# Attention by pairs of heads in a six-layer kernel, with four score banks and the bias added in PSUM

## Chip, cores and metric

The kernel runs on one core of a Trainium2 chip. The metric is the device time of one execution in microseconds (us), lower is better. The core's engines are TensorE (PE, matrix products), VectorE (DVE), ScalarE (ACT), GpSimd (POOL) and SyncE (SP, which issues the weight loads). They run side by side and meet at semaphores. Matrix products are written to PSUM, which has eight banks here: `acc0` to `acc3`, `prod0`, `prod1`, `stat0`, `stat1`.

## What is computed

A stack of six layers on 256 tokens of width 1024, all in float32: each layer is half a SwiGLU feed-forward (2816 hidden), a mixer, and another half feed-forward. The mixers are, in order, gated linear attention, neighbourhood attention (NA), latent attention (MLA), gated linear attention, and twice four branches, of which two are attentions. Four mixers hold a softmax attention, and those are what the change touches:

```python
# NA, 16 heads of 64: a bias per pair of positions, NEG_INF outside the window
s = jnp.einsum('bqhd,brkhd->bhqrk', q_r, k_blk) * NA_HEAD_DIM ** -0.5
p = softmax(where(mask, s + bias, NEG_INF));  o = p @ v
# MLA, 16 heads: 64 plain and 32 rotated dimensions, no mask, no bias
s = jnp.einsum('bqhd,bkhd->bhqk', q, k) * (64 + 32) ** -0.5
p = softmax(s);  o = p @ v                       # v has 64 columns a head
# branches: 4 sliding-window heads with a bias and a sink
p = exp(s - m) / (sum(exp(s - m)) + exp(sink - m))
# and 4 forgetting heads: s + (cum_q - cum_k), causal
```

## The kernel before

All weights come as slabs of 1 MB (`raw`, three buffers), each of which ScalarE rounds to its high part (`split`, L853) and VectorE reduces to the low rest (`low_of`, L1132). A projection multiplies high by high, high by low and low by high in fp32r (`three`, L404 to L406) into a `prod` bank; the feed-forward sums go to the `acc` banks. The attention has no weights: it runs in plain float32, where every matmul is issued as two passes of the array.

The order of the work is written out by hand, one instruction stream for each engine. The mixers `na`, `mla` and `branches` of each engine first run the projections and norms of queries, keys and values, then call that engine's `attention`, and then the output projection. In all of them 256 queries are two tiles of 128 (`tt`), and 256 keys are two tiles (`kt`).

`attention` on TensorE (L565 to L594) loops over `i` in `heads + 3` steps. Step `i` waits for the scaled probabilities of head `i-2` (`p_ready`, L570), writes the scores of head `i` to `acc[i % 2]` (L575; two query tiles, one term each in NA, two terms in MLA with 64 and with 32 rows, three terms in the forgetting heads with 64, 4 and 4 rows), transposes the probabilities of head `i-2` to `acc[2 + h % 2]` (L582), and multiplies the values of head `i-3` by the transposed probabilities (L592) into one half of a `stat` bank: even heads fill partitions 0 to 63, odd ones 64 to 127. A head with an even number has its queries and keys on partitions 0 to 63, one with an odd number on 64 to 127 (`half64`).

VectorE's `attention` (L1317) does for head `i`: scale and bias of the scores (L1330), from `acc` to a `logits` buffer, then the maximum (L1334 or L1337); in MLA a maximum of `acc` (L1325) and its product with the scale (L1326). Then for head `i-1`: the reciprocal of the sum (L1345) and two multiplications of the probabilities (L1347), which signal `p_ready`. Every other step it takes the low rest of a finished pair of outputs (`low_out`, L1360). In the branches it also does the gates' remaining work between steps (`operands`, L1667).

ScalarE's `attention` (L918) copies the transposed probabilities out of PSUM (L926), computes the exponentials with their sums (L932, from `logits`, or in MLA from `acc`), the sink's exponential (L935), and the high part of a pair of outputs (L941).

Before NA's attention VectorE still has two slab rests to do, and before that of the branches one gate and a slab rest (`lows`).

Of the kernel before, what the change touches and what calls it, by code (L numbers as in the profile page):

```python
# [15 lines left out]
P = 128  # L16
# [114 lines left out]
def build(nc, W, PRM, CST, START, RPB, XIN, OUT, TOE_ROWS, TOE):  # L131
    ctx = ExitStack()
    with ctx:
# [35 lines left out]
        small = sb("small", [P, 4, 8])  # L169
# [107 lines left out]
        def half64(h):  # L277
            return slice(64 * (h % 2), 64 * (h % 2) + 64)
# [19 lines left out]
        def attention_buffers(at, rest, i):  # L298
            return [[bits(at, 0), bits(at, 1)], [bits(at, 2), bits(at, 3)], [bits(rest, i), bits(rest, i + 1)]]
# [93 lines left out]
        def _(pe):  # L393
# [171 lines left out]
            def attention(kind, heads, scores, values):  # L565

                _, probs, probsT = buffers[kind]
                for i in range(heads + 3):
                    if 2 <= i < heads + 2:
                        pe.wait_ge(p_ready, c.up(p_ready))  # L570
                    if i < heads:
                        for tt in range(TT):
                            pairs = scores(i, tt)
                            for n, (lhs, rhs) in enumerate(pairs):
                                last = nc.tensor.matmul(acc[i % 2][:, tt, :], lhs, rhs, start=(n == 0),  # L575
                                                        stop=(n == len(pairs) - 1))
                        last.then_inc(s_done, 1)
                    if 2 <= i < heads + 2:
                        h = i - 2
                        for kt in range(TT):  # L580
                            for tt in range(TT):
                                last = nc.tensor.transpose(acc[2 + h % 2][:, kt, tt * P:(tt + 1) * P],  # L582
                                                           probs[h % 2][:, tt, kt * P:(kt + 1) * P], ident)
                        last.then_inc(t_done, 1)
                    if i >= 3:
                        h = i - 3
                        if h % 2 == 0 and h >= 4:
                            pe.wait_ge(ot_ready, ot_base + h // 2 - 1)
                        pe.wait_ge(pt_ready, c.up(pt_ready))
                        half = slice(64 * (h % 2), 64 * (h % 2) + 64)  # L590
                        for kt in range(TT):
                            last = nc.tensor.matmul(stat[h // 2 % 2][half, 0, :], values(h, kt), probsT[h % 2][:, kt, :],  # L592
                                                    start=(kt == 0), stop=(kt == TT - 1))
                        last.then_inc(pv_done, 1)  # L594

# [230 lines left out]
        def _(act):  # L826
# [91 lines left out]
            def attention(heads, scale, kind, sink=None):  # L918

                out = xh if kind == "branches" else oh  # L920
                logits, probs, probsT = buffers[kind]
                tables("natural_log_exp_and_others")
                for i in range(heads + 3):
                    if 2 <= i < heads + 2:
                        act.wait_ge(t_done, c.up(t_done))
                        nc.scalar.activation(probsT[i % 2][:, :, :], acc[2 + i % 2][:, :, :], ACT.Copy).then_inc(pt_ready, 1)  # L926
                    if i < heads:
                        act.wait_ge(logits_ready, c.up(logits_ready))
                        st = small[:, i % 2, :]
                        src = acc[i % 2] if scale else logits[i % 2]  # L930
                        for tt in range(TT):
                            last = nc.scalar.activation(probs[i % 2][:, tt, :], src[:, tt, :], ACT.Exp, bias=st[:, tt:tt + 1],  # L932
# [1054 lines left out]
```

## Time and profile before

| | us |
|---|---|
| median of 3 runs | 3887.76 (3886.63 to 3892.89) |
| the profiled execution | 3889.2 |
| its span in the trace | 3887.4 |

| engine | busy us | share of the span |
|---|---|---|
| TensorE, matmul | 3635.3 | 94% |
| TensorE, weight load | 3445.8 | 89% |
| VectorE | 2591.0 | 67% |
| ScalarE | 1495.6 | 38% |
| GpSimd | 7.0 | 0% |

The profile is of one execution. A matmul's record is longer than the distance to the next, since matmuls are pipelined; the distance between starts is what a matmul costs in a row of them. The granted clock is TensorE's share of its full speed: 1.00 is 2.4 GHz, 0.50 is 1.2 GHz; over the span it is 0.952. In every view a line number is that of the code above, an arrow names what ended the idle time, and the shapes are partitions times elements. A float32 matmul of the attention appears as two records, one for each pass.

### The profile page before, as it was taken

To read this page: it belongs to the slowest core of one execution; us is meant where nothing else is said; L and a number is where in the kernel's file an instruction comes from. 1 tells how busy PE (TensorE), PEld (TensorE's weight loads), DVE (VectorE), ACT (ScalarE), POOL (GpSimd) and SP (SyncE) were. 2 spreads that over 40 slices of the span, in tenths; PEclk is the share of its full clock that TensorE was granted. 3 is DMA by queue.
4 is the path that set the end of the run, shared out by engine and by line. 5 is a ranking of instruction groups with operands and counts; after the bars stand their busy time and mean duration, and the time that the engine had idled before them with its cause. 6 is when DMAs were issued, how large, how long until landed. Compare 5 with 4: busy or idle time off the path is not lost.

```text
span 3887.4 us, 65961 instructions
## 1 busy us (share of the span) xinstructions
PE 3635.3 (94%) x27625; PEld 3445.8 (89%) x27625; DVE 2591.0 (67%) x2987; ACT 1495.6 (38%) x1446; POOL 7.0 (0%) x6
## 2 busy tenths in 40 slices
PE   8998899997999986999999889999888999988899
PEld 8997799995899986499999879999867999987799
DVE  7678767676667667266767876766766666676565
ACT  4343334343434343243434233434343343444243
POOL 0000000000000000000000000000000000000000
PEclk9999999998999998699999989999988999998899
DMA  6542374542354442035555225454432545543154
GB/s 240 183 179 82 120 216 173 183 152 98 109 183 176 180 162 87 0 141 183 176 180 182 90 88 191 175 185 173 163 120 85 186 173 186 183 161 141 65 184 162
DMA packets 98919, 592.68 MB, mean 152 GB/s; under 512 B 25684, under 2 KB 26836, under 8 KB 27736
## 3 DMA queue, kind: packets, MB, share of 16 engines
q1 hardware_dynamic: 97280, 586.41, 42.3%
q10 hardware_dynamic: 1496, 4.20, 0.3%
q8 instruction: 109, 1.79, 0.2%
q14 instruction: 34, 0.28, 0.0%
HBM read 588.47 MB, written 2.11 MB: 152 GB/s over the span
## 4 chain that ended last, share of the span: by engine, by line
PE 80%; DVE 13%; issue 4%; ACT 3%; DMA 1%; SPq 0%; DVEq 0%; ACTq 0%
PE prod L404 18%; PE prod L406 18%; PE prod L405 18%; PE acc L404 7%; PE acc L406 6%; PE acc L405 6%; PE acc L575 3%; DVE low L1132 3%; ACT high L853 2%; DVE work L1426 1%; PE stat L592 1%; DVE work L1627 1%; DVE work L1419 1%; PE acc L582 1%; DVE newt L1166 1%
## 5 line engine op out<-in xcount | busy, mean ns | idle before, releaser
L404 PE MATMUL prod<-xh,high 128*128 128x256 f32 x5968 | 1710.9, 287 | 45.9 <-DVE gs L1690 12.8
L405 PE MATMUL prod<-xl,high 128*128 128x256 f32 x5968 | 1691.5, 283 | 0.0
L406 PE MATMUL prod<-xh,low 128*128 128x256 f32 x5968 | 1684.9, 282 | 0.0
L1132 DVE TENSOR_TENSOR low<-raw,high 128x2048 fp32r<-128x2048 f32 x537 | 1231.9, 2295 | 559.6 <-ACT high L853 555.3
L853 ACT ACTIVATE high<-raw 128x2048 fp32r<-128x2048 f32 x550 | 1047.7, 1908 | 950.0 <-PE prod L406 486.1
L404 PEld LDWEIGHTS prod<-xh,high 128*128 128x128 f32 x5968 | 1128.4, 189 | 64.3 <-issue 25.6
L406 PEld LDWEIGHTS prod<-xh,low 128*128 128x128 f32 x5968 | 1137.8, 191 | 0.0
L405 PEld LDWEIGHTS prod<-xl,high 128*128 128x128 f32 x5968 | 1131.4, 190 | 4.1 <-issue 3.1
L404 PE MATMUL acc<-ends,high 128*128 128x256 f32 x2112 | 597.8, 283 | 0.4 <-DVE low L1132 0.4
L405 PE MATMUL acc<-ends,high 128*128 128x256 f32 x2112 | 596.6, 282 | 0.0
L406 PE MATMUL acc<-ends,low 128*128 128x256 f32 x2112 | 591.9, 280 | 0.0
L406 PEld LDWEIGHTS acc<-ends,low 128*128 128x128 f32 x2112 | 401.7, 190 | 0.0
L405 PEld LDWEIGHTS acc<-ends,high 128*128 128x128 f32 x2112 | 396.4, 188 | 0.0
L404 PEld LDWEIGHTS acc<-ends,high 128*128 128x128 f32 x2112 | 394.9, 187 | 0.6 <-issue 0.6
L910 ACT ACTIVATE sg<-gs 128x512 f32<-128x512 f32 x120 | 76.0, 634 | 561.0 <-DVE gs L1281 561.0
L1281 DVE TENSOR_TENSOR gs<-prod,rstd 128x512 f32<-128x512 f32 x120 | 83.0, 691 | 162.7 <-PE prod L406 162.6
L575 PE MATMUL acc<-work 64*128 64x256 f32 (+1 forms) x256 | 109.9, 563 | 51.3 <-DVE work L1347 42.8
L1247 DVE TENSOR_TENSOR sg<-sg,gs 128x512 f32<-128x512 f32 x132 | 92.1, 698 | 93.2 <-ACT sg L910 84.0
L575 PEld LDWEIGHTS acc<-work 64*128 64x128 f32 (+1 forms) x256 | 52.4, 253 | 108.6 <-DVE work L1347 60.2
L404 PE MATMUL prod<-ends,high 128*128 128x256 f32 x384 | 114.0, 297 | 30.7 <-DVE ends L1458 19.0
L405 PE MATMUL prod<-ends,high 128*128 128x256 f32 x384 | 112.8, 294 | 0.0
L406 PE MATMUL prod<-ends,low 128*128 128x256 f32 x384 | 112.7, 293 | 0.0
(194 smaller groups left out, 2772.6 us busy)
## 6 DMA issues: line engine op xcount, KB each, us to landing
raw<-stream SPq DMA_DIRECT2D x550, 1024.0 KB, 4.8
work<-rpb SPq DMA_DIRECT2D x16, 256.0 KB, 6.6
work<-bias_shifted ACTq DMA_DIRECT2D x2, 1024.0 KB, 5.3
cst<-consts SPq DMA_DIRECT2D x1, 1122.0 KB, 11.5
x<-x_in SPq DMA_DIRECT2D x1, 1024.0 KB, 5.0
raw<-stream SPq DMA_DIRECT2D x2, 512.0 KB, 7.0
work<-bias_by_distance ACTq DMA_DIRECT2D x2, 512.0 KB, 4.6
bias_shifted<-work ACTq DMA_DIRECT2D x1, 1024.0 KB, 5.8
```

The costliest lines, as they stand in the source:

```text
L404: nc.tensor.matmul(out, wh, ah, start=start, stop=False, **kw)
L405: nc.tensor.matmul(out, wh, al, start=False, stop=False, **kw)
L406: return nc.tensor.matmul(out, wl, ah, start=False, stop=stop, **kw)
L575: last = nc.tensor.matmul(acc[i % 2][:, tt, :], lhs, rhs, start=(n == 0), stop=(n == len(pairs) - 1))
L582: last = nc.tensor.transpose(acc[2 + h % 2][:, kt, tt * P:(tt + 1) * P], probs[h % 2][:, tt, kt * P:(kt + 1) * P], ident)
L592: last = nc.tensor.matmul(stat[h // 2 % 2][half, 0, :], values(h, kt), probsT[h % 2][:, kt, :], start=(kt == 0), stop=(kt == TT - 1))
L853: nc.scalar.activation(high[:, s % HIGH, :], raw[:, s % RAW, :], ACT.Copy).then_inc(high_ready, 1)
L910: nc.scalar.activation(sg[:, :, :], gs[:, :, :], ACT.Sigmoid).then_inc(sig_ready, 1)
L1132: v.tensor_tensor(low[:, s % LOW, :], raw[:, s % RAW, :], high[:, s % HIGH, :].bitcast(F32), ALU.subtract).then_inc(low_ready, 1)
L1166: link(v.tensor_tensor(t, t, w, ALU.mult))
L1247: v.tensor_tensor(sg[:, :, :], sg[:, :, :], gs[:, :, :], ALU.mult).then_inc(vec_step, 1)
L1281: v.tensor_tensor(gs[:, :, :], prod[0][:, :, :], over(rstd[:, :], 2), ALU.mult).then_inc(evac, 1)
```

## The change

- The three `attention` functions loop over pairs of heads. On TensorE, step `i` writes the scores of pair `i`, then the values of pair `i-3`, then the transposes of pair `i-2`. Scores and values are issued alternately for the two heads of the pair: term by term for scores, key tile by key tile for values.
- Scores go to four banks, `acc[2 * (i % 2) + u]`. They wait for the exponentials of pair `i-2` (`exp_done`), no longer for its scaled probabilities. Transposes go to `prod[u]`; for that TensorE waits at the start for all projections to be taken out of `prod` (`evac`).
- The probabilities have four buffers, and `small` eight rows. The `logits` buffers are gone: scale and bias are written back to the same PSUM bank, from which the maximum and the exponentials are read.
- In MLA the scale goes into the norm of the queries (`variance(..., factor)`), so that the maximum is taken with `negate=True` and no product follows.
- Output copies and `low_out` follow each pair step, the last three `low_out` after the loop. `operands(i)` is now called at pair steps.

```diff
-        small = sb("small", [P, 4, 8])
+        small = sb("small", [P, 8, 8])
...
-            return [[bits(at, 0), bits(at, 1)], [bits(at, 2), bits(at, 3)], [bits(rest, i), bits(rest, i + 1)]]
+            return [bits(at, j) for j in range(4)], [bits(rest, i), bits(rest, i + 1)]
...
@@ TensorE, in place of L567 to L594
+                probs, probsT = buffers[kind]
+                pairs = heads // 2
+                pe.wait_ge(evac, n_prod[0])
+                exps = c.now(exp_done)
+                c.up(exp_done, heads)
+                for i in range(pairs + 3):
+                    if i < pairs:
+                        if i >= 2:
+                            pe.wait_ge(exp_done, exps + 2 * (i - 1))
+                        terms = len(scores(2 * i, 0))
+                        for tt in range(TT):
+                            for n in range(terms):
+                                for u in range(2):
+                                    lhs, rhs = scores(2 * i + u, tt)[n]
+                                    last = nc.tensor.matmul(acc[2 * (i % 2) + u][:, tt, :], lhs, rhs, start=(n == 0),
+                                                            stop=(n == terms - 1))
+                                    if tt == TT - 1 and n == terms - 1:
+                                        last.then_inc(s_done, 1)
+                    if i >= 3:
+                        pair = i - 3
+                        if pair >= 2:
+                            pe.wait_ge(ot_ready, ot_base + pair - 1)
+                        pe.wait_ge(pt_ready, c.up(pt_ready, 2))
+                        for kt in range(TT):
+                            for u in range(2):
+                                last = nc.tensor.matmul(stat[pair % 2][half64(u), 0, :], values(2 * pair + u, kt), probsT[u][:, kt, :],
+                                                        start=(kt == 0), stop=(kt == TT - 1))
+                        last.then_inc(pv_done, 1)
+                    if 2 <= i < pairs + 2:
+                        for u in range(2):
+                            pe.wait_ge(p_ready, c.up(p_ready))
+                            for kt in range(TT):
+                                for tt in range(TT):
+                                    last = nc.tensor.transpose(prod[u][:, kt, tt * P:(tt + 1) * P],
+                                                               probs[(2 * (i - 2) + u) % 4][:, tt, kt * P:(kt + 1) * P], ident)
+                            last.then_inc(t_done, 1)
@@ ScalarE, in place of L922 to L941
+                pairs = heads // 2
+                for i in range(pairs + 3):
+                    for u in range(2):
+                        h = 2 * i + u
+                        if 2 <= i < pairs + 2:
+                            act.wait_ge(t_done, c.up(t_done))
+                            nc.scalar.activation(probsT[u], prod[u][:, :, :], ACT.Copy).then_inc(pt_ready, 1)
+                        if i < pairs:
+                            act.wait_ge(logits_ready, c.up(logits_ready))
+                            st = small[:, h % 4, :]
+                            for tt in range(TT):
+                                last = nc.scalar.activation(probs[h % 4][:, tt, :], acc[h % 4][:, tt, :], ACT.Exp, bias=st[:, tt:tt + 1],
+                                                            accum_out=st[:, 2 + tt:3 + tt])
...
+                            last.then_inc(exp_done, 1)
                     if i >= 3:
                         act.wait_ge(pv_done, c.up(pv_done))
...
+                        nc.scalar.activation(out[:, i - 3, :], stat[(i - 3) % 2][:, 0, :], ACT.Copy).then_inc(ot_high, 1)
@@ VectorE, in place of L1319 to L1355
+                def largest(h):
+                    st, mx, b = small[:, h % 4, :], small[:, 4 + h % 4, 0:2], acc[h % 4][:, :, :]
+                    dve.wait_ge(s_done, c.up(s_done))
+                    if bias is not None:
+                        added = bias(h)
+                        k = added.shape[-1]
+                        rows = b.rearrange("p a (r k) -> p (a r) k", k=k)
+                        link(v.scalar_tensor_tensor(rows, rows, scale, added, ALU.mult, ALU.add))
...
+                        v.tensor_reduce(st[:, 0:2], b, AX_X, ALU.max, negate=True).then_inc(logits_ready, 1)
+
+                def shares(h):
+                    st = small[:, h % 4, :]
+                    dve.wait_ge(exp_done, c.up(exp_done))
...
+                    link(v.reciprocal(st[:, 6:8], st[:, 2:4]))
+                    for tt in range(TT):
+                        last = v.tensor_scalar(probs[h % 4][:, tt, :], probs[h % 4][:, tt, :], st[:, 6 + tt:7 + tt], None, ALU.mult)
+                    last.then_inc(p_ready, 1)
+
+                for i in range(pairs + 1):
+                    for u in range(2):
+                        if i < pairs:
+                            largest(2 * i + u)
+                        if i >= 1:
+                            shares(2 * (i - 1) + u)
+                    if i >= 4:
+                        low_out(i - 4, out)
                     if between:
                         between(i)
+                for pair in range(pairs - 3, pairs):
+                    low_out(pair, out)
...
-                    qs = (variance(2 * T, NOPE + ROPE), variance(T, NOPE + ROPE))
+                    scale = 1.0 if keys else float(NOPE + ROPE)
+                    qs = (variance(2 * T, NOPE + ROPE, scale), variance(T, NOPE + ROPE, scale))
```

## Rows read from the trace of the kernel before

**Rows 1.** The page's chain of waits: share of the span by line.

```profile
PE prod L404 18%; PE prod L406 18%; PE prod L405 18%; PE acc L404 7%; PE acc L406 6%; PE acc L405 6%; PE acc L575 3%; DVE low L1132 3%; ACT high L853 2%; DVE work L1426 1%; PE stat L592 1%; DVE work L1627 1%; DVE work L1419 1%; PE acc L582 1%; DVE newt L1166 1%
```

**Rows 2.** Window table: us, busy of PE, PEld, DVE, ACT, POOL; PEclk, DMA, GB/s.

```profile
932.60:998.70 66.10, 48.53 (x193) 27.46 (x192) 41.79 (x92) 31.11 (x89) 0.00 (x0) 0.85 0.11 41
957.30:998.70 41.40, 33.47 (x151) 18.85 (x150) 26.35 (x66) 21.90 (x64) 0.00 (x0) 1.00 0.00 0
1557.50:1661.80 104.30, 100.59 (x257) 47.10 (x257) 27.59 (x88) 27.35 (x88) 0.00 (x0) 0.62 0.00 0
1557.50:1605.70 48.20, 45.79 (x94) 20.97 (x94) 10.44 (x33) 10.36 (x35) 0.00 (x0) 0.50 0.00 0
2877.00:2934.90 57.90, 44.64 (x131) 23.89 (x129) 27.24 (x60) 19.59 (x52) 0.00 (x0) 0.65 0.12 44
3570.40:3628.00 57.60, 44.35 (x130) 23.67 (x129) 27.21 (x60) 19.81 (x52) 0.00 (x0) 0.64 0.13 45
```

**Rows 3.** Chain in order of time in NA: start us, length us, what.

```profile
961.33 0.70 DVE work L1330
...
962.06 0.69 DVE small L1337
...
962.85 0.62 DVE work L1347 x2
...
963.52 1.14 PE acc L575 x4
...
964.69 0.70 DVE work L1330
```

**Rows 4.** Timeline in NA: start us, length us, engine, line, operation, tiles, idle before.

```profile
960.03 0.42 DVE L1360 TENSOR_TENSOR ends<-stat,ends 128x256 fp32r<-128x256 f32 x1
...
961.23 0.66 PE L582 MATMUL acc<-cst,work 128*128 128x128 f32 x4
...
961.81 1.08 PE L592 MATMUL stat<-work 128*64 128x256 f32 x4
961.98 0.60 ACT L926 ACTIVATE work<-acc 128x512 f32<-128x512 f32 x1 [1.46 <-PE acc L582]
...
962.78 0.51 ACT L932 ACTIVATE work<-work,small 128x256 f32<-128x256 f32 x1 [0.20 <-DVE small L1337]
```

**Rows 5.** Timeline where NA's attention begins.

```profile
932.66 1.14 PE L575 MATMUL acc<-work 64*128 64x256 f32 x8
...
938.75 0.68 DVE L1330 SCALAR_TENSOR_TENSOR work<-acc,work 128x512 f32<-128x512 f32 x1
```

**Rows 6.** Chain in order of time in NA at half clock.

```profile
946.55 2.07 PE acc L575 x4
...
949.66 1.90 PE stat L592 x4
```

**Rows 7.** Chain in order of time in MLA at half clock.

```profile
1589.99 4.59 PE acc L575 x8
1594.58 1.04 PE acc L582 x4
1595.62 1.90 PE stat L592 x4
```

**Rows 8.** Chain in order of time in MLA at full clock.

```profile
1609.62 2.57 PE acc L575 x8
```

**Rows 9.** Groups by line in MLA: maximum taken from PSUM.

```profile
L1325 DVE TENSOR_REDUCE small<-acc 128x2 f32<-128x512 f32 x16 | 11.1, 691 | 71.2 <-PE acc L575 71.2
```

**Rows 10.** Groups by line in NA: maximum taken from SBUF.

```profile
L1337 DVE TENSOR_REDUCE small<-work 128x2 f32<-128x512 f32 x16 | 11.0, 686 | 0.5
```

**Rows 11.** Chain in a branches layer: scores of forgetting heads, half and full clock.

```profile
2914.19 6.29 PE acc L575 x12
...
2923.43 3.37 PE acc L575 x12
```

**Rows 12.** Timeline in a branches layer: TensorE's second scores.

```profile
2888.83 2.07 PE L575 MATMUL acc<-work 64*128 64x256 f32 x4 [10.63 <-DVE work L1347]
```

More of the change, by code:

```diff
@@ L565, in attention @@
             def attention(kind, heads, scores, values):
[L567 to L571, printed above, removed]
-                        for tt in range(TT):
[L573 to L579, printed above, removed]
-                        for kt in range(TT):
[L581 to L593, printed above, removed]
-                        last.then_inc(pv_done, 1)
@@ L916, in ffn, with attention @@
                 ahead(s0 + FFN_SLABS - 1)
-            def attention(heads, scale, kind, sink=None):
+            def attention(heads, kind, sink=None):
                 out = xh if kind == "branches" else oh
-                logits, probs, probsT = buffers[kind]
+                probs, probsT = buffers[kind]
                 tables("natural_log_exp_and_others")
[L923 to L932, printed above, removed]
-                                                        scale=scale or 1.0, accum_out=st[:, 2 + tt:3 + tt])
-                        if sink is not None and i < SWA_HEADS:
-                            last = nc.scalar.activation(st[:, 4:6], st[:, 0:2], ACT.Exp, bias=sink(i))
-                        last.then_inc(exp_done, 1)
@@ new lines, in attention @@
+                pairs = heads // 2
[11 more added lines that the diff above has]
+                                                            accum_out=st[:, 2 + tt:3 + tt])
+                            if sink is not None and h < SWA_HEADS:
+                                last = nc.scalar.activation(st[:, 4:6], st[:, 0:2], ACT.Exp, bias=sink(h))
+                            last.then_inc(exp_done, 1)
@@ L993, in na @@
                 ahead(s + 8, 4)
-                attention(NA_HEADS, None, "na")
+                attention(NA_HEADS, "na")
                 complete(gain, evac, s + 12)
@@ L1148, in half_low, with variance @@
                                 ALU.subtract).then_inc(signal, 1)
-            def variance(width, n):
+            def variance(width, n, factor=1.0):
                 q = n_stat[0] % 2
@@ new lines, in attention @@
+                probs, _ = buffers[kind]
+                pairs = heads // 2
+                def largest(h):
[6 more added lines that the diff above has]
+                        link(v.scalar_tensor_tensor(rows, rows, scale, added, ALU.mult, ALU.add))
+                    if sink is not None and h < SWA_HEADS:
+                        link(v.tensor_reduce(mx, b, AX_X, ALU.max))
+                        v.tensor_scalar(st[:, 0:2], mx, sink(h), -1.0, ALU.max, ALU.mult).then_inc(logits_ready, 1)
+                    else:
+                        v.tensor_reduce(st[:, 0:2], b, AX_X, ALU.max, negate=True).then_inc(logits_ready, 1)
```

54 lines of the change are left out of this document (9 added, 45 removed).

## Prediction

> **What bounds the kernel now.** I read the page's chain of waits first: most of the span is TensorE in the fp32r projections (the lines of `three`), which this change does not touch. The attention lines L575, L582 and L592 hold about 5% of the chain, with the VectorE work between them [rows 1]. So I went to the stages. The window table gives four attention stretches: neighbourhood attention (NA) 66.1 us, MLA 104.3, and the two branches layers 57.9 and 57.6, together 285.9 us [rows 2]. DMA is idle in most of them and the slabs for the next projection are already split, so time saved here should reach the end.
>
> They have three different limits. In NA at full clock a serial loop between two engines sets the pace: bias add 961.33, maximum 962.06, shares 962.85, next scores 963.52, and the next bias add 964.69, 3.36 us a head, of which 2.2 VectorE and 1.1 TensorE [rows 3]. `wait_ge(p_ready)` ahead of `scores` makes that loop: TensorE does not issue scores until VectorE has scaled the head two before. In MLA TensorE never stops: 4.59 us scores, 1.04 transposes, 1.90 values a head, 7.53 in all at half clock [rows 7]; the granted clock is 0.50 for the first 48.2 us [rows 2]. The branches mix both; at half clock a forgetting head's scores take 6.29 us, at full 3.37 [rows 11].
>
> **The scores.** Heads 2i and 2i+1 lie in rows 0-63 and 64-127 of the array. At the start of NA two heads' scores are queued together: eight passes in 1.14 us [rows 5], where four passes of one head later take 1.14 as well [rows 3]. Two heads overlap completely when nothing stands between them. The change makes every pair like that, so I price a pair's scores at one head's: 1.14 us at full clock, 2.07 at half [rows 6]. The other end is no overlap, twice as much; I take full overlap because a row shows it for the same shapes.
>
> The Trainium skill (TensorE: Matmul & The Clock Gate, Part 3) says that tiles in different row groups overlap but that matmuls start in program order. By that rule heads issued one after the other would not start together, as they do in [rows 5]; the row decides, and in alternating order both would overlap anyway, with 5 pass times where 4 are counted here, some 2 us on MLA.
>
> MLA's scores change tile height (64 rows, then 32) four times a head; 4.59/4 = 1.15 us each [rows 7], and even its first two heads cannot overlap. After, all terms of equal height of a pair stand together: four such steps a pair and not eight, each with two heads at once. A pair's scores are then 4.59 us at half clock, 2.57 at full [rows 7, 8]. The forgetting heads' two 4-row terms use the same rows for both heads and stay serial; of 6.29 us, 2 x 1.15 is the 64-row term and 4.0 the others. A pair has 2 x (1.15 + 2.0 + four further passes at 0.45) = 9.9 us for 12.6, at full clock 5.1 for 6.7 [rows 11].
>
> **Transposes and values.** Transposes stay 1.04 us a head at half clock [rows 7] and about 0.6 at full (four recorded in 0.66, [rows 4]); only their bank moves to `prod`. A pair's values, alternating between column halves 0-63 and 64-127 of one bank, have no overlapping example in this trace: 1.90 us (both at once) to 3.8 (serial) at half clock [rows 6], 1.08 to 2.0 at full [rows 4]. I take overlap, by nearness to the row halves. (The Trainium skill, TensorEngine Tiling (Array Packing), Key Properties, has tiles running in parallel; no run here shows it for columns.) A TensorE pair is thus 1.14+1.2+1.08 = 3.4 (4.3 serial) us at full clock in NA, 2.07+2.08+1.9 = 6.1 (8.0) at half; in MLA 2.57+1.2+1.0 = 4.8 (5.8), or 4.59+2.08+1.9 = 8.6 (10.5).
>
> **VectorE and ScalarE.** With two pairs of lead and four score banks VectorE no longer waits for the scores it has just released. Its step a pair in NA is two heads at 2.14 us (961.33 to the end of 962.85) plus `low_out` 0.42 = 4.7 us [rows 3, 4]. MLA drops one tiny VectorE product a head by putting the factor 96 into the variance: no gain, since TensorE is the bound; a VectorE pair there, without bias adds, is 4.7 - 2 x 0.7 = 3.3. ScalarE has four exponentials of 0.51, two copies of 0.60 and small ones (sums, output) that I put at 0.6, 3.8 us a pair [rows 4], below either bound. The bias add now writes its PSUM bank and the maximum reads PSUM. No row shows VectorE writing PSUM; reading PSUM and writing SBUF is 691 ns. Bounds of -0.1 to +0.1 us a bias add, times 32, are -3 to +3 us on the path; I take zero. A maximum from PSUM takes 691 ns [rows 9] against 686 from SBUF [rows 10]: 32 x 5 ns is nothing.
>
> The Trainium skill (VectorE: DVE Perf Modes, the TRN2 errata) charges 62 cycles more for a PSUM source than for an SBUF one. This speaks against the change: 32 maxima x 65 ns would be an estimated 2 us. The two rows disagree with it.
>
> **Waits added.** `evac` at the start, because `prod` now takes transposes: behind it stand the first two pairs' scores, for which VectorE waits; VectorE is busy with slab lows until 938.75 anyway [rows 5], so it is hidden, and would cost about 2 us a stage without them. `exp_done` before scores holds transposes and values queued behind it, but it is for the pair two back and long done when VectorE or TensorE is the bound. `pt_ready` of values now stands ahead of the transposes; ScalarE has a scores time to finish the copies: hidden, or 0.5 us a pair at full clock in MLA (0 to 4 us, taken as 0).
>
> **The sum, by stage.** NA: VectorE starts 6.1 us into the stage, eight steps of 4.7 = 37.6, then transposes, copy, values, copy and `low_out` 3.3: 47. TensorE begins at half clock after its idle time, as now; there its 6.1 us outrun the 4.7, I add 2: 49 for 66.1, gain 17. MLA: 8 x 4.8 + 4 for fill and tail = 42 at full clock. I let the first 20 us be at half clock, +10: 52 for 104.3, gain 52. Branches: TensorE is idle until 2888.8, when the first shares come [rows 12]; I keep that. All at half clock, 2 x 9.9 + 4 x 2.08 + 4 x 1.9 + 2 = 38, end 2926.5 for 2934.9, gain 8. At full clock VectorE decides: its 27.2 us of work in the stage [rows 2] all stay, with some 10 of waits at the two ends 37, gain 21. Between them 14, twice 28. Together 17 + 52 + 28 = 97 us off the profiled execution's 3889.2 (span 3887.4): 3792; the median is 1.4 lower, so 3791.
>
> **The clock** is the largest unknown. What the rows show: NA reaches 1.00 at 957.3 after working gaplessly at half clock since about 946 and keeps it for 41.4 us, although TensorE then waits each head; MLA stays at 0.50 for 48.2 us though TensorE is busy 45.8 of them [rows 2]. The differences are 32-row terms and the gaps of height changes. After the change the same passes run in about 0.57 of the time, two at once, denser than NA's today. That is why I let it rise.
>
> The Trainium skill (TensorE: Matmul & The Clock Gate, Part 1) says activity releases the half clock. MLA contradicts that as it stands; by the rule the outcome is rival F below.
>
> **Rivals.**
> (A) As above, 3791: 0.42.
> (B) Column halves do not overlap: NA is still covered (4.3 under 4.7), MLA loses 8 x 1.0, each branches layer 3: 3791 + 14 = 3805: 0.15. For: no row shows it. Against: row halves do.
> (C) The clock stays at half in MLA and the forgetting heads. MLA 8 x 8.6 + 6 = 75, gain 29; branches 2 x 8; NA 17: 62 us, 3826: 0.27. For: the 48.2 us. Against: denser work.
> (D) The change does not do what it says, scores do not overlap in alternation. NA hardly suffers (4.5 against 4.7), MLA 8 x 7.4 + 12 = 71, gain 33, branches 8 each: 3889 - 66 = 3822: 0.04.
> (E) Slower: each switch between row or column halves drains the array as MLA's height changes do, 1.15 us for two passes at half clock [rows 7], and the clock stays there. NA's pair is 4.6 + 2.1 + 4.6 = 11.3 us, stage 98; MLA 9.2 + 2.1 + 4.6 = 15.9, stage 133; branches +10 each: +81 us, 3969. It turns slower where a TensorE pair passes about 7 us in NA and 12.5 in MLA. Against: eight passes in 1.14 us. 0.03.
>
> (F) MLA runs at full clock from its first scores on, 42 us and not 52: 3781, 0.09. For: its first scores are packed as densely as any later ones. Against: the stage starts at half clock now [rows 2]. (The same is what the Trainium skill's page on TensorE, named above, would lead to.)
>
> **Range.** All at full clock gives 19 + 62 + 42 = 123 us, 3765, the lower end. Upward C is taken in, with half the price of B at half clock (15): 3840. Left out are C with B in full, and E. A alone reaches from 3765 to 3808. About 0.2% (8 us) can be told from no change: faster 0.96, same 0.01, slower 0.03.
>
> **What would show it.** Scores of a pair: eight passes in 1.14 us. MLA's scores: 16 passes in 2.6 (4.6) us for two heads, and its granted clock. Values: eight passes in 1.1 or in 1.9 us. NA: bias adds of a pair every 4.7 us with no wait for L575's successor. The bias add's mean near 691 ns. Wrong would be a MLA stage above 75 us, a VectorE wait for scores in the middle of NA, or a changed time outside the four stages.

## The result, and the profile after

The changed kernel takes 3799.21 us (median of four runs, 3797.88 to 3802.74) where the kernel before takes 3889.13 (3886.63 to 3892.89): ratio 0.9769, 95% interval 0.9752 to 0.9786. The prediction was 3791 with a range of 3765 to 3840. The profiled execution after is 3797.88 us long, its span 3796.1 for 3887.4 before, so 91.3 us went.

Where they went is read by one rule for all kernels here: an attention stage runs from the start of the last projection matmul before it to the start of the first one behind it. For MLA this takes in some 45 us of norms and small sums ahead of the scores, the same in both kernels.

| us | before | after | gone |
|---|---|---|---|
| NA | 66.4 | 48.5 | 17.8 |
| MLA | 149.9 | 94.1 | 55.8 |
| branches, first | 58.0 | 48.4 | 9.7 |
| branches, second | 57.8 | 45.1 | 12.7 |
| all the rest | 3555.4 | 3560.0 | -4.6 |

The window table of the changed kernel (NA, the first projections behind it, MLA in two parts, the forgetting heads of the first branches layer, the second branches layer; columns as in [rows 2]):

```profile
933.50:981.70 48.20, 29.08 (x193) 18.73 (x192) 40.68 (x92) 28.36 (x89) 0.00 (x0) 0.89 0.14 52
981.70:986.70 5.00, 4.98 (x29) 4.98 (x30) 0.00 (x0) 0.00 (x0) 0.00 (x0) 0.66 0.01 3
1542.00:1559.00 17.00, 16.95 (x62) 8.16 (x62) 6.61 (x18) 5.93 (x23) 0.00 (x0) 0.50 0.01 1
1559.00:1590.90 31.90, 27.58 (x198) 15.86 (x196) 17.82 (x54) 19.94 (x67) 0.00 (x0) 1.00 0.00 1
...
2818.60:2849.00 30.40, 29.09 (x88) 18.21 (x88) 16.49 (x47) 9.11 (x33) 0.00 (x0) 0.50 0.00 1
...
3492.70:3534.70 42.00, 31.01 (x129) 19.95 (x129) 24.34 (x58) 18.18 (x52) 0.00 (x0) 0.67 0.14 51
```

In NA, TensorE's busy time fell from 48.5 us [rows 2] to 29.1 with the same 193 matmul records: most of that is the overlap of pairs, a part of it the higher granted clock (0.89 for 0.85). VectorE's stayed near 41, now of a stage of 48.2. In MLA the granted clock is 0.50 for 17 us, not 48.2, and then 1.00 to the end. In the first branches layer it is 0.50 while the forgetting heads run.

The chain of waits of the changed kernel in NA, in order of time (start us, length us, what); it answers to [rows 3]:

```profile
959.11 0.62 DVE acc L1338
...
959.75 0.69 DVE small L1343
...
960.55 0.62 DVE work L1352 x2
961.16 0.62 DVE acc L1338
...
963.22 0.33 DVE ends L1371
963.55 0.61 DVE acc L1338
...
972.10 0.34 DVE ends L1371
...
972.48 1.97 PE stat L592 x8
974.46 1.06 PE prod L600 x4
975.54 1.09 ACT work L937 x2
```

The scores are gone from the chain: VectorE goes from bias add to maximum to shares of two heads and `low_out` without a wait, and a pair takes 4.44 us (959.11 to 963.55). Before, one head took 3.36. But after VectorE's last step that has scores to work on, which ends at 972.10, a tail begins in which TensorE, ScalarE and VectorE work by turns, until the next projection at 981.72.

The same view in MLA (L581 scores, L600 transposes, L592 values, L937 ScalarE's copy of the transposes); it answers to [rows 7, 8]:

```profile
1542.05 13.91 PE acc L581 x48
...
1557.85 3.13 PE acc L581 x16
1560.99 1.01 PE stat L592 x8
1562.00 1.02 PE prod L600 x8
1563.03 2.53 PE acc L581 x16
...
1576.72 2.53 PE acc L581 x16
1579.24 1.01 PE stat L592 x8
...
1588.90 1.10 PE stat L592 x8
```

Sixteen score passes, two heads, take 2.53 us at full clock, where eight passes of one head took 2.57 [rows 8]. Eight passes of values take 1.01.

### The profile page after: what moved, and what is told of

Same layout as the page of the kernel before. It is cut to its first block, busy times and chain, and to the rows that moved or that the text cites. A ratio compares the mean times of both kernels' runs of the same rounds, so it can differ in the third digit from the quotient of the medians.

```text
span 3796.1 us, 65923 instructions
## 1 busy us (share of the span) xinstructions
PE 3547.5 (93%) x27625; PEld 3418.4 (90%) x27625; DVE 2586.0 (68%) x2971; ACT 1488.5 (39%) x1446; POOL 7.4 (0%) x6
## 4 chain that ended last, share of the span: by engine, by line
PE 79%; DVE 13%; issue 4%; ACT 4%; DMA 1%; SPq 0%; DVEq 0%; ACTq 0%
PE prod L404 19%; PE prod L405 18%; PE prod L406 18%; PE acc L404 7%; PE acc L405 7%; PE acc L406 7%; DVE low L1140 3%; ACT high L861 2%; PE acc L581 2%; DVE work L1437 1%; DVE work L1639 1%; DVE work L1430 1%; DVE newt L1174 1%; DVE newt L1173 1%; PE stat L592 1%
## 5 line engine op out<-in xcount | busy, mean ns | idle before, releaser
L404 PE MATMUL prod<-xh,high 128*128 128x256 f32 x5968 | 1711.5, 287 | 46.2 <-DVE gs L1702 13.2
L878 ACT ACTIVATE xh<-x,prm 128x256 fp32r<-128x256 f32 x140 | 63.6, 502 | 121.1 <-DVE x L1242 115.9
L404 PEld LDWEIGHTS prod<-ends,high 128*128 128x128 f32 x384 | 78.2, 204 | 34.3 <-DVE ends L1469 21.3
```

What stands on the lines that cost most here:

```text
L404: nc.tensor.matmul(out, wh, ah, start=start, stop=False, **kw)
L878: return nc.scalar.activation(xh[:, k, :], x[:, k, :], ACT.Identity, scale=par(gain, k))
```

## The experiments

All of them are read against the kernel before that ran beside them (3888.6 to 3890.5 us). The stages are measured as in the table above.

**The lead without the pairs.** The kernel before, with its order of heads, its banks and its VectorE work.

```diff
+                exps = c.now(exp_done)
+                c.up(exp_done, heads)
                 for i in range(heads + 3):
-                    if 2 <= i < heads + 2:
-                        pe.wait_ge(p_ready, c.up(p_ready))
+                    if 2 <= i < heads:
+                        pe.wait_ge(exp_done, exps + i - 1)
...
                     if 2 <= i < heads + 2:
                         h = i - 2
+                        pe.wait_ge(p_ready, c.up(p_ready))
```

> The kernel before with one part of the change: scores of head i wait for the exponentials of head i-2 (exp_done) and the wait for the scaled probabilities (p_ready) stands ahead of the transposes. No pairs, no four banks, no alternation. Theory 'three limits': only NA has the serial loop that this opens; there TensorE's own 2.7 us a head (1.06 + 0.59 + 1.08) becomes the pace in place of 3.36, about 10 us off the stage of 66; MLA stays near 104 us at half clock, since TensorE never stopped there; the branches 1 to 4 us each; in all 12 to 18 us, 3871 to 3877. Rival 'the lead is what counts': most of the 90 us come back here, 3815 or below.

Measured: 3854.98 us, ratio 0.9919 (0.9903 to 0.9936). NA 54.6, MLA 131.2, branches 54.9 and 53.1. That is 33.8 us off, where 12 to 18 were expected and the rival wanted more than 70: neither forecast held. NA and the branches are about as expected, but MLA, expected to keep its time, lost 18.7 us. The profiled execution is the fastest of four (3849.57 to 3863.01 us), so its stages may show more than the others had. Window table of this kernel's MLA scores, and its chain of waits:

```profile
1545.70:1584.00 38.30, 38.27 (x78) 17.52 (x78) 8.90 (x28) 8.45 (x29) 0.00 (x0) 0.50 0.00 0
1584.00:1629.50 45.50, 44.47 (x179) 22.51 (x178) 18.70 (x60) 18.41 (x59) 0.00 (x0) 1.00 0.00 1
```

```profile
1587.61 2.50 PE acc L577 x8
1590.11 0.58 PE acc L585 x4
1590.70 1.01 PE stat L595 x4
```

The kernel before, where its clock first rises in MLA (TensorE's timeline):

```profile
1604.98 2.94 PE L575 MATMUL acc<-work 64*128 64x256 f32 x8
1607.85 0.66 PE L582 MATMUL acc<-cst,work 128*128 128x128 f32 x4
1608.44 1.08 PE L592 MATMUL stat<-work 128*64 128x256 f32 x4
1609.62 2.57 PE L575 MATMUL acc<-work 64*128 64x256 f32 x8
```

At half clock TensorE is the bound and, after the first two heads, does not wait. At full clock VectorE's answer to one head's scores comes 1.7 us after them, but transposes and values fill nearly all of that: the old `p_ready` wait stops TensorE from 1609.52 to 1609.62, 0.11 us. The clock fell back each time it had risen (0.62 over the stage, [rows 2]). With the lead that wait is gone, and the clock stays at 1.00 for 45.5 us. Over the whole stage TensorE's idle time falls from 2.7 us (2.4 of them behind the first two heads) to 0.1; the other 16 us of the 18.7 are clock. So in this execution the lead gives MLA clock, not only NA its overlap with VectorE. How so short a wait could matter to the clock is not shown, and three stretches speak against it as the cause by itself: NA waits longer in every head at 1.00 [rows 2, 3], the kernel with one height below has the same 0.11 us in every head at 1.00, and the pairs without the alternation below fall back to 0.50 with no wait at all.

**The pairs without the alternation.** The changed kernel, with the scores and values of a pair issued head after head.

```diff
-                        for tt in range(TT):
-                            for n in range(terms):
-                                for u in range(2):
+                        for u in range(2):
+                            for tt in range(TT):
+                                for n in range(terms):
...
-                        for kt in range(TT):
-                            for u in range(2):
+                        for u in range(2):
+                            for kt in range(TT):
```

> The changed kernel, but scores and values of a pair issued one head after the other, all else as changed. Theory 'TensorE overlaps neighbours in its queue as long as the tile height does not change': NA's pair of scores still takes 1.14 us and its stage stays at 48 us; a pair's values still 1.08 us or a little more. In MLA each head changes height four times again, so a pair's scores take 5.1 us at full clock (9.2 at half) in place of 2.53 (4.6): the stage is 65 to 72 us if the clock still rises, 105 if it doesn't; forgetting pairs cost 6.7 (12.6) in place of 5.1 (9.8). Total 3825 to 3865. Rival 'matmuls start in program order': scores in NA take 2.1 us a pair and values 1.9, with the same in MLA and the branches; total 10 to 20 us more than that.

Measured: 3858.42 us, 0.9924 (0.9907 to 0.9940). NA 47.2, MLA 140.1, branches 52.4 each. The total lies in the range expected, and MLA's 95 us from its first scores on lie between the 65 to 72 and the 105 priced, since the clock rises only in part. NA loses nothing. Its TensorE timeline (L592 values, L581 scores):

```profile
959.45 1.09 PE L592 MATMUL stat<-work 128*64 128x256 f32 x8 [2.49 <-DVE ends L1371]
...
961.49 1.14 PE L581 MATMUL acc<-work 64*128 64x256 f32 x8
```

Eight passes of scores in 1.14 us and eight of values in 1.09, so the rival of program order fell: where both heads use tiles of one height, two heads overlap in either order. In MLA they do not (chain of waits, then window table):

```profile
1581.49 9.17 PE acc L581 x16
```

```profile
1539.00:1593.60 54.60, 54.59 (x118) 25.65 (x119) 12.75 (x35) 10.18 (x37) 0.00 (x0) 0.50 0.00 0
1593.60:1634.00 40.40, 36.30 (x141) 19.30 (x139) 12.45 (x37) 15.84 (x51) 0.00 (x0) 0.75 0.00 1
```

9.17 us for a pair's scores is twice 4.59. The alternation matters where the height changes, and there it is worth 46 us of MLA and 59 us of the kernel (3858.4 to 3799.2). These 46 us are shorter passes and more clock together; here the clock went up and down between 0.50 and 1.00 from 1593.5 on, and it did so before TensorE's first recorded wait, at 1624.58. The Trainium skill (TensorEngine Tiling (Array Packing), Key Properties) says that a change of tiling mode drains the engine, while tiles of one mode work in parallel. The trace agrees: between two heads' equal tiles nothing is lost, at each change of height the other head's overlap ends.

**The transposes first.** The tail of the stages, measured in all of them, suggested a change of its own: in each step the transposes of pair i-2 stand ahead of the values of pair i-3, with four buffers of transposed shares instead of two.

```diff
-                    if i >= 3:
-                        pair = i - 3
...
                     if 2 <= i < pairs + 2:
                         for u in range(2):
...
+                    if i >= 3:
+                        pair = i - 3
...
+                                last = nc.tensor.matmul(stat[pair % 2][half64(u), 0, :], values(2 * pair + u, kt), probsT[(2 * pair + u) % 4][:, kt, :],
...
-                            nc.scalar.activation(probsT[u], prod[u][:, :, :], ACT.Copy).then_inc(pt_ready, 1)
+                            nc.scalar.activation(probsT[(h - 4) % 4], prod[u][:, :, :], ACT.Copy).then_inc(pt_ready, 1)
```

> The changed kernel with each step's transposes issued ahead of the values, and four buffers for the transposed probabilities (at the end of each stage the changed kernel has TensorE wait for copies, then transposes, copies and values one after the other). Theory 'the tail was priced too low': the stretch from VectorE's last shares to the first projection shrinks from 9.2 us to 3 to 4 in NA, MLA and the branches lose about 5 us each; total 15 to 22 us off, 3777 to 3785. Rival 'the waits only move': the transposes now hold back values, VectorE's steps get longer, less than 5 us off or slower.

Measured: 3782.43 us, 0.9724 (0.9707 to 0.9740). The total is as expected, its parts are smaller. NA 46.0, MLA 91.4, branches 44.4 and 41.0: 2.5, 2.6, 3.9 and 4.1 us less than the changed kernel, where some 5 each were expected; that is 13.2 of the 13.8 us between the two profiled spans. NA's tail is 7.1 us (974.80 to 981.86) for 9.6, not 3 to 4. Its chain at the end of NA:

```profile
975.96 1.91 PE stat L604 x8
977.87 1.15 PE prod L594 x8
979.02 1.93 PE stat L604 x16
...
980.97 0.39 ACT ends L953
```

The ScalarE copies (1.09 us each time) that stood in the chain between transposes and values are gone from it; they run beside the other matmuls.

**The forgetting sums on two groups of rows.** The two 4-row terms of each forgetting head used rows 0 to 3 for all heads. Here the sums are computed a second time on partitions 32 to 35, and odd heads read those.

```diff
...
+                four = slice(32 * (g % 2), 32 * (g % 2) + FOX_HEADS)
+                select = cst[four, CONSTS["select"][0] + g:CONSTS["select"][0] + g + 1]
...
-                        (br_cum[0:FOX_HEADS, tok], con("select", g, 1, FOX_HEADS).to_broadcast([FOX_HEADS, T])),
-                        (con("select", g, 1, FOX_HEADS).to_broadcast([FOX_HEADS, P]), br_ncum[0:FOX_HEADS, :])]
+                        (br_cum[four, tok], select.to_broadcast([FOX_HEADS, T])),
+                        (select.to_broadcast([FOX_HEADS, P]), br_ncum[four, :])]
...
```

> The changed kernel, with the forget gates' sums kept a second time on partitions 32 to 35, from which the odd head of a pair takes its two 4-row terms. The computed result is the same. Theory 'the 4-row terms are serial because both heads use the same rows of the array': a forgetting pair's scores fall from 9.79 us to 6.3 at half clock, or from 5.1 to 3.4 at full; over two pairs in two layers 7 to 14 us, 3785 to 3792. Rival 'they are serial for another reason, such as the broadcast operand': 9.8 us stay, total within 2 us of the changed kernel.

Measured: 3788.70 us, 0.9743 (0.9726 to 0.9759), as expected. A forgetting pair's scores in the changed kernel, and in this one (chain of waits, both at half clock):

```profile
2818.62 9.79 PE acc L581 x24
```

```profile
2819.16 6.39 PE acc L582 x24
```

The pairs' 4-row terms were indeed serial; in row groups of their own they overlap. The branches take 41.6 and 39.9 us for 48.4 and 45.1.

**The waits filled.** Does MLA start at half clock because TensorE waits before it? Five matmuls on constants were put ahead of the stage's wait for its last norm, and behind the second pair's scores in the other stages.

```diff
+            def fill(n):
+                for _ in range(n):
+                    nc.tensor.matmul(prod[0][:, :, :].rearrange("p a t -> p (a t)"), con("blk64"), cst[:, 0:2 * T], start=True, stop=True)
...
+                    if i == 1 and kind != "mla":
+                        fill(5)
...
+                pe.wait_ge(evac, n_prod[0])
+                fill(5)
                 pe.wait_ge(norm_ready, c.up(norm_ready))
```

> The changed kernel, with five float32 matmuls of constants (their results are overwritten) where TensorE waits ahead of MLA's first scores, and five after the first two pairs' scores in NA and in the branches. Theory 'each stage starts at half clock because TensorE has just been idle, and that half clock costs what the passes say': MLA starts at or near full clock, its stage falls from 48.9 us to 42 to 45; in the branches the first forgetting pair's scores fall from 9.8 towards 5.1 us, 3 to 8 us a layer; NA within 2 us, since VectorE covers it; in all 8 to 20 us, 3780 to 3791. Rival 'the kind of attention work decides, not the idle time before it': the clock falls all the same, total within 3 us of the changed kernel or up to 10 us above it, as the five matmuls delay the scores.

Measured: 3799.12 us, 0.9767 (0.9750 to 0.9783): no difference from the changed kernel. Window table, around MLA's start and at NA's:

```profile
1534.00:1541.00 7.00, 6.90 (x17) 3.62 (x15) 5.70 (x11) 1.98 (x4) 0.00 (x0) 0.82 0.00 0
1541.00:1543.20 2.20, 0.00 (x0) 0.00 (x0) 2.06 (x5) 0.00 (x0) 0.00 (x0) 1.00 0.00 0
1543.20:1560.00 16.80, 16.73 (x60) 8.10 (x60) 6.63 (x19) 5.72 (x22) 0.00 (x0) 0.50 0.00 1
...
936.50:955.00 18.50, 13.40 (x78) 7.89 (x80) 18.05 (x33) 9.49 (x33) 0.00 (x0) 1.00 0.31 114
```

TensorE was busy for 6.90 of the 7 us before 1541, the clock was at 1.00 in the gap, and the first scores ran at 0.50 all the same. The theory's forecast failed, and MLA took 94.1 us as without the filler. But the filler did not fill the whole wait: 2.4 us of idle time were left ahead of the scores (1540.90 to 1543.27), so that such a gap matters is not excluded. The same holds for the first branches layer: 2.7 us were left, its first forgetting pair took 9.7 us and the layer 48.4. The second layer took 43.2 for 45.1. In NA the filler did keep the clock at 1.00, and the stage took 48.5 us as without it. So half clock at NA's start costs nothing, because VectorE sets the pace.

**Height by height.** The changed kernel, with the loop over the terms outside the one over query tiles: two changes of height a pair instead of four.

```diff
-                        for tt in range(TT):
-                            for n in range(terms):
+                        for n in range(terms):
+                            for tt in range(TT):
...
-                                    last = nc.tensor.matmul(acc[2 * (i % 2) + u][:, tt, :], lhs, rhs, start=(n == 0),
-                                                            stop=(n == terms - 1))
+                                    last = nc.tensor.matmul(acc[2 * (i % 2) + u][:, tt, :], lhs, rhs, start=(n == 0 and tt == 0),
+                                                            stop=(n == terms - 1), skip_group_check=True)
```

> The changed kernel, with a pair's terms issued by tile height across both query tiles (all 64-row terms, then all 32-row or 4-row ones), so that a pair changes height twice and not four times. The result is the same. Theory 'each change of height costs a fixed gap, 0.63 us for two passes against 0.43 without it at full clock, 1.15 against 0.86 at half': a pair's scores in MLA fall from 2.53 to 2.1 us at full clock (4.6 to 4.0 at half), 3 to 5 us on the stage; a forgetting pair by 0.6 to 0.8 us, 1 to 2 us a layer; total 5 to 9 us off, 3790 to 3794. Rival 'the gap belongs to the 32-row tiles, however often they come': under 2 us.

Measured: 3796.31 us, 0.9758 (0.9742 to 0.9774); the interval overlaps the changed kernel's 0.9752 to 0.9786, so the runs do not tell the two apart, and the 2.9 us between the medians lie between the 5 to 9 of the theory and the rival's 2. The trace does tell them apart, in the scores (its chain in MLA, one pair at half and one at full clock):

```profile
1558.53 4.01 PE acc L581 x16
...
1565.75 2.13 PE acc L581 x16
```

2.13 us a pair for 2.53, so two changes of height cost 0.40 us at full clock, and the rival fell. MLA is 92.7 for 94.1, the branches 45.5 and 42.2 for 48.4 and 45.1, each with some 7 us less at half clock; NA, whose instructions are the same, was 51.9 in this execution, with the clock at 0.52 from 957.2 to 964.0 and 0.51 from 974.3 to its end.

**One height.** The kernel before, in which MLA's 32-row term is replaced by the 64-row term a second time. This leaves the rotated part out of MLA's scores; the number of matmuls stays.

```diff
-                                         (ml_qr[part32(h), h // 4, tt * P:(tt + 1) * P], ml_kr[part32(h), h // 4, :])],
+                                         (ml_qn[half64(h), h // 2, tt * P:(tt + 1) * P], ml_kn[half64(h), h // 2, :])],
```

> The kernel before with one edit: the second term of MLA's scores, 32 rows high, is replaced by the first, 64-row term again (left out: the rotated part of MLA's scores; the count of matmuls stays). Question: what keeps MLA's clock low in the kernel before, the alternation of tile heights in its scores or the waits of its serial loop? Tile heights: the eight score passes of a head take about 3.6 us at half clock and 1.9 at full one instead of 4.59 and 2.57, the clock rises within some 20 us of the stage's start and stays, and the stage is near 60 us instead of 104. Serial loop: the passes are shorter by the same amounts, but at full clock TensorE then waits still longer for ScalarE and VectorE (2.4 us a head instead of 1.7), the clock falls back or never rises, and the stage is 85 to 95 us. Other stages as before.

Measured, in one execution: 3857.69 us beside 3888.62; MLA 114.4 for 149.9. Window table and chain in MLA:

```profile
1560.60:1580.70 20.10, 17.73 (x46) 11.86 (x47) 5.48 (x17) 5.06 (x18) 0.00 (x0) 0.50 0.00 1
1580.70:1629.80 49.10, 46.90 (x212) 29.68 (x210) 22.09 (x71) 21.74 (x70) 0.00 (x0) 1.00 0.00 1
```

```profile
1584.25 2.00 PE acc L575 x8
...
1587.94 2.00 PE acc L575 x8
```

The clock rises after 20 us and stays, although TensorE waits 0.11 us in every head here too (1587.84 to 1587.94; the rest of the 1.7 us between two heads' scores is transposes and values). The tile heights' side is right on the clock. Its stage of 60 us came out as 69 from first scores to next projection: a head takes 3.69 us at full clock, nearly all of it TensorE's own work. Eight passes take 3.79 us at half and 2.00 at full clock, where 3.6 and 1.9 were expected and the kernel before has 4.59 and 2.57. The 2.4 us of waiting a head that the serial side forecast are not there.

**Two and three edits together.** The changed kernel with the transposes first and the doubled sums, and then with the height order too.

> The two edits transposes_first and fox_rows together, on the changed kernel. They act on different stretches (the end of every stage; the forgetting heads' scores), so theory 'the gains add' says 17 + 10 us off the changed kernel, 3772 (3768 to 3776). Rival 'they share a wait': with shorter scores the transposes wait for VectorE and the tail gives part back, 3778 or above.

Measured: 3767.59 us, 0.9683 (0.9667 to 0.9699). The two edits gain 16.8 and 10.5 us alone and 31.6 together, slightly more than expected. In the four stages of the profiled executions it is 13.2, 12.0 and 25.9 us: there the gains add, and what is over lies outside the stages.

> The changed kernel with the three edits that each gained: a pair's transposes ahead of the older pair's values (four buffers of transposed shares), the forget sums doubled on partitions 32 to 35 so that the even heads' terms start on one row and the odd ones' on another, and the terms taken height by height over the query tiles. The first two together were 3767.6 us; the third took 2.9 us from the changed kernel alone, most of it in MLA and the branches. If the gains add: 3762 to 3766 us. Rival: where transposes come first TensorE no longer sets the pace, and the third edit gives nothing: 3766 to 3769 us.

Measured: 3764.33 us (five runs, 3761.99 to 3765.66), 0.9680 (0.9667 to 0.9693). The number lies where the gains would add, but the kernel before beside it was 1.9 us faster than beside the two edits, and the intervals overlap: that the third edit adds anything is not shown. This is the fastest kernel of the study, 34.9 us under the changed one. Window table of its NA and MLA, from the first scores on:

```profile
935.40:977.80 42.40, 27.73 (x193) 17.29 (x193) 39.04 (x90) 27.03 (x89) 0.00 (x0) 0.92 0.13 50
1536.80:1581.30 44.50, 43.34 (x257) 27.40 (x257) 24.24 (x72) 25.91 (x88) 0.00 (x0) 0.76 0.00 1
```

VectorE is busy 39.0 of 42.4 us in NA and TensorE 43.3 of 44.5 in MLA; there is little idle time left on the engine that bounds each.

## Why the prediction was right

The sum was 97 us, the trace has 91.3; the sign, the overlap of pairs and the size held. The stages are off by +0.8, +3.8, -5.7 and -4.6 us (NA, MLA, branches, rest), which cancel in part, and that is luck. By its own steps:

**The scores.** Held. In alternation a pair takes 1.14 us in NA, and in MLA 2.53 for the 2.57 priced. Rival D fell (its 3889 - 66 is 3823, not 3822, which decides nothing). The prediction's sentence that two heads overlap "completely when nothing stands between them" is true of NA; the pairs without alternation showed that in MLA it needs the alternation. The forgetting pair measured 9.79 us for 9.9.

**The values.** Priced at 1.08 us with no row for it, and measured so. Groups by line in NA of the changed kernel (TensorE's and VectorE's of the attention):

```profile
L1338 DVE SCALAR_TENSOR_TENSOR acc<-acc,work 128x512 f32<-128x512 f32 x16 | 11.1, 691 | 0.0
L1343 DVE TENSOR_REDUCE small<-acc 128x2 f32<-128x512 f32 x16 | 11.1, 691 | 0.5
L592 PE MATMUL stat<-work 128*64 128x256 f32 x64 | 9.6, 423 | 10.3 <-DVE ends L1371 7.4 <-ACT work L937 3.0
```

Rivals B and E fell: column halves overlap, and no switch between halves drains anything.

**The bias add in PSUM.** 691 ns, as taken; the maximum 691 too, against 686 from SBUF [rows 10]. The Trainium skill's 62 further cycles for a PSUM source (VectorE: DVE Perf Modes, the TRN2 errata) are not in the maximum, 5 ns apart; the bias add reads PSUM before and after, so it has no row from SBUF to compare.

**The waits added.** `evac` cost nothing in NA: VectorE's first bias add begins 6.41 us after the last projection matmul's start in both kernels (932.34 to 938.75 and 933.18 to 939.59). In the first branches layer it is 7.8 us in both. One wait was not priced: values wait for `low_out` two pairs back, 7.4 us in NA in the row above. While VectorE is the bound it delays nothing. Where the tail begins it does: TensorE stands idle for 2.33 us until the `low_out` of 972.10 is done, though the copies that these values need were done 0.7 us earlier (971.74). And the next transposes, whose shares are ready at 972.10, stand behind those values until 974.39.

**NA: 17 priced, 17.8 measured, by luck: the errors in it cancel.** VectorE's eight steps took 32.5 us (939.59 to 972.10) for 37.6: without waits a bias add follows after 0.62 us and not 0.70, and the first steps have no `low_out`. The tail was priced at 3.3 us and is 9.6 (972.10 to 981.72). The 3.3 hold one round of transposes, copies and values. With two pairs of lead, two such rounds follow behind the values of a third pair, one engine after the other, and the last pair's shares fall in this stretch too; this is the mis-sized term. The 2 us for half clock at the start were not spent, as the filled waits showed.

**MLA: 52 priced, 55.8 measured.** From the first scores to the next projection it took 48.9 us (1542.05 to 1590.91) for the 52 priced. A pair is 4.56 us (four from 1560.99 to 1579.24) for 4.8, 1.9 us less over eight. TensorE's idle time is 4.3 us, all of it in the tail, for the 4 priced as fill and tail. The remaining 8 us are half clock, priced at 10; it lasted some 17 us for the 20 let. Rival C fell here, and F too. One part of the mechanism was missing: the prediction has MLA limited by TensorE's work alone, yet the order of waits alone took 18.7 us off it with the same scores, most of them by the clock.

**The branches: 28 priced, 22.3 measured.** This is the step that failed in size. I took the middle between all half and all full clock. In the first layer the clock was 0.50 for the 30.4 us of the forgetting heads; there the all-half price was 8 and the trace has 9.7. In the second it rose earlier, 12.7. Rival C is right in this place. At half clock the serial 4-row terms are the bound, and then the tail is, as the two experiments on them showed.

**The rest: 0 priced, -4.6 measured.** A changed time outside the four stages is on the prediction's own list of signs against it. A part of it is that the clock falls in NA's thin tail and the first projections run at 0.66 [window table above]; TensorE before went into them at 1.00 [rows 2]. But with the transposes first there is no such fall, and the rest is 3559.4 all the same. Over all eleven profiled executions here, whose matmuls are the same in that part, it runs from 3554.0 to 3563.3 us, and it goes with the granted clock. Outside the stages the clock was 0.50 for 172 us before and for 196 after; the three executions with the least of it (172 to 185 us) have the three shortest rests (3554.0 to 3555.4), the one with the most (210 us) the longest. Of the 24 us more, 10 lie ahead of NA's attention, where no instruction was changed. So it looks like scatter of the clock between executions; what sets it is not shown.

**The clock in MLA.** The prediction let it rise "because denser". What the runs show, by MLA's window tables:

- before: 0.50 for 48.2 us, then up and down; 61% of a head's TensorE time in scores that change height (4.59 of 7.53), and a wait of 0.11 us a head while it is up
- with the lead alone: 0.50 for 38.3 us, then 1.00; the same scores, no waits
- with one height: 0.50 for 20.1 us, then 1.00; the wait of 0.11 us a head, no height changes
- pairs head after head: 0.50 for 54.6 us, then up and down (0.75); no waits until the tail, and 71% of the time in such scores (9.17 of 12.98)
- the change: 0.50 for 17 us, then 1.00; no waits until the tail, 55% (4.64 of 8.44)

So the clock stayed up without the wait at 55 and 61%, and with the wait at 0%; it fell back with the wait at 61%, and without any wait at 71%. The waits alone do not hold it down, and they are not needed for it to fall. The share of height-changing scores does not order the time to the first rise either: 0% has 20.1 us and 55% has 17, and the height-by-height order, with fewer changes, still had half clock some 20 us into its scores. Each of these is one execution. What counts as work for the clock is open, and so is why MLA starts at half clock.

## What to carry to other kernels

Issue the matmuls of two heads in alternation where their terms differ in tile height, and give each head its own group of rows also for the smallest terms: overlap within one height is free in any order, across a change of height it is lost. When a serial loop is loosened, price the drain at its end too, since each stage of lead adds a round over all engines there, and let the work that another engine must still finish (transposes) go ahead of the work that only ends (values). Read the granted clock stage by stage beside the waits: an edit that left TensorE's work as it was and took 2.6 us of waiting out of MLA moved that stage by 18.7 us, most of it through the clock, which a list of waits would not have shown.

## What the runs showed of the hardware

Two changes of tile height within a pair's sixteen score passes cost 0.40 us at full clock (2.53 to 2.13), and with one height throughout eight passes take 2.00 us instead of 2.57. Matmuls on the two column halves of the array, 64 columns each, run at once: eight passes in 1.08 us, the time of four. Two heads' tiles of one height overlap also when all of one head's passes are issued ahead of the other's (eight passes in 1.14 us in both orders). The 4-row terms of two heads are serial on the same rows and overlap on partitions 0 to 3 and 32 to 35 (9.79 and 6.39 us a pair at half clock). TensorE can work without a gap for 54.6 us, busy in 54.59 of them, and be granted 0.50 throughout: a busy engine alone does not bring the full clock.
